# Two thirds of the modulation product moved from TensorE to GpSimd, and inputs laid out by the host

## What is computed

```python
def adaln_params(cond, w_mod, b_mod):
    m = jax.nn.silu(cond) @ w_mod + b_mod          # w_mod: 1024 x 6144
    return jnp.split(m, N_MOD, axis=-1)            # N_MOD = 6 parts of 1024
...
    sh1, sc1, g1, sh2, sc2, g2 = [m[:, None, :] for m in adaln_params(c, w_mod, b_mod)]
    csh1, csc1, cg1, csh2, csc2, cg2 = adaln_params(c_ctx, w_mod, b_mod)
    hc = rmsnorm(xc, n1) * (1 + csc1) + csh1
    ...
    h = rmsnorm(x, n1) * (1 + sc1) + sh1
    q, k, v, gb, gcv, u, ga, gv = split_proj(h @ w_in)
    ...
    x = x + g1 * merge_branches(y_attn, y_conv, ga, gv, w_mix_out)
    h2 = rmsnorm(x, n2) * (1 + sc2) + sh2
    x = x + g2 * peer(h2, pw_q, p_keys, p_u, p_v)
```

## Time and profile before

| | |
|---|---|
| runs | 1750.57, 1737.38, 1738.53 us; median 1738.53 |
| profiled execution | 1739.62 us, of which the span of instructions is 1737.8 us |
| busy | PE 1536.9 us, DVE 1044.2, ACT 774.4, POOL 276.6 |
| mean granted clock of PE | 0.953 of full speed |
| DMA | 431.63 MB, 248 GB/s over the span |

### The profile page before, as it was taken

One profiled execution on the slowest core, in us unless ns is written; L12 is line 12 of the kernel. 1 busy time (PEld: TensorE's weight loads), 2 busy tenths in 40 slices (PEclk: granted clock), 3 DMA queues, 4 the chain that ended last, 5 costly groups with the idle time before them and its releaser, 6 DMA issues.

```text
span 1737.8 us, 23096 instructions
## 1 busy us (share of the span) xinstructions
PE 1536.9 (88%) x8485; PEld 1124.3 (65%) x8485; DVE 1044.2 (60%) x2092; ACT 774.4 (45%) x1654; POOL 276.6 (16%) x260
## 2 busy tenths in 40 slices
PE   7899999969898898788877779888999988899997
PEld 4699559835444333222222249788999986899997
DVE  3445326466666666776665447535777766467774
ACT  2444333334444444444444353444555545455553
POOL 0000000035444443344444300000000000000000
PEclk9899999989999999999999989879999998899997
DMA  7345443399999999999999934303555531245551
GB/s 280 122 167 173 170 152 139 130 401 422 421 421 421 421 421 421 422 421 421 422 421 422 421 145 144 123 1 146 178 185 183 180 121 49 73 156 183 184 178 73
DMA packets 60724, 431.63 MB, mean 248 GB/s; under 512 B 6764, under 2 KB 7393, under 8 KB 8673
## 3 DMA queue, kind: packets, MB, share of 16 engines
q0 software_dynamic: 36864, 268.45, 37.2%
q1 hardware_dynamic: 22618, 159.51, 26.0%
q10 hardware_dynamic: 1159, 2.58, 0.5%
HBM read 429.47 MB, written 1.05 MB: 248 GB/s over the span
## 4 chain that ended last, share of the span: by engine, by line
PE 45%; DMA 20%; ACT 7%; DVE 5%; issue 2%; POOL 0%; ACTq 0%; POOLq 0%; DVEq 0%; SPq 0%
PE banks L595 18%; DMA arena<-in_peer_uv,experts 14%; PE banks L952 12%; PE banks L1058 7%; DMA tok_a<-in_peer_uv,experts 2%; DMA tok_b<-in_peer_uv,experts 2%; PE banks L834 2%; ACT diag L1330 2%; DVE wlow L1518 2%; PE banks L808 1%; PE banks L673 1%; PE banks L627 1%; ACT scores L1234 1%; ACT whigh L1099 1%; PE banks L792 1%
## 5 line engine op out<-in xcount | busy, mean ns | idle before, releaser
L952 PE MATMUL banks<-arena,diag 128*128 128x512 f32 x824 | 406.9, 631 | 99.1 <-ACT diag L1330 99.1
L952 PEld LDWEIGHTS banks<-arena,diag 128*128 128x128 f32 x824 | 150.9, 196 | 342.7 <-ACT diag L1330 207.9
L1871 DVE CUSTOM_DVE_ANT_0 arena<-arena,scores 128x1024 f32<-128x1024 f32 x206 | 252.6, 1226 | 191.7 <-DMA arena<-in_peer_uv,experts 190.9
L1518 DVE TENSOR_TENSOR wlow<-wring,whigh 128x1024 fp32r<-128x1024 f32 x234 | 275.4, 1219 | 128.9 <-ACT whigh L1099 128.9
L1472 POOL DMA_INDIRECT arena<-in_peer_uv,experts x206 | 221.9, 1077 | 648.3 <-DVE experts L1835 343.8
L1099 ACT ACTIVATE whigh<-wring 128x1024 fp32r<-128x1024 f32 x234 | 233.9, 1048 | 139.3 <-DMA wring<-in_w_qkv_a 33.6
L595 PE MATMUL banks<-f_high,whigh 128*128 128x256 f32 x720 | 206.0, 286 | 15.5 <-DVE f_low L1554 10.0
L595 PE MATMUL banks<-f_low,whigh 128*128 128x256 f32 x720 | 204.6, 284 | 0.0
L595 PE MATMUL banks<-f_high,wlow 128*128 128x256 f32 x720 | 204.5, 284 | 0.0
L1322 ACT ACTIVATE dots<-dots 128x1 f32<-128x1 f32 x256 | 51.4, 201 | 297.1 <-DVE dots L1871 296.6
L595 PE MATMUL banks<-a_high,whigh 128*128 128x256 f32 x552 | 165.8, 300 | 12.6 <-DVE a_low L1526 6.9
(11 more groups left out here) (251 smaller groups left out, 2525.6 us busy)
## 6 DMA issues: line engine op xcount, KB each, us to landing
wring<-in_w_up SPq DMA_DIRECT2D x44, 1024.0 KB, 4.8
wring<-in_w_mod SPq DMA_DIRECT2D x24, 1024.0 KB, 5.0
wring<-in_w_down SPq DMA_DIRECT2D x22, 1024.0 KB, 4.9
wring<-in_w_in SPq DMA_DIRECT2D x17, 1024.0 KB, 4.9
wring<-in_w_qkv_a SPq DMA_DIRECT2D x12, 1024.0 KB, 5.1
wring<-in_peer_w_q SPq DMA_DIRECT2D x8, 1024.0 KB, 4.9
wring<-in_w_mix_out SPq DMA_DIRECT2D x4, 1024.0 KB, 4.8
wring<-in_w_o_a SPq DMA_DIRECT2D x4, 1024.0 KB, 5.0
```

Source lines behind the costliest of these rows:

```text
L952: mm = nc.tensor.matmul(banks[:, 2 + 2 * b + half, :], diag[:, n % DIAGS, :], ring[n % RING][:, D + half * 512:D + (half + 1) * 512], star ...
L1518: V.tensor_tensor(low, w, high.bitcast(F32), ALU.subtract).then_inc(w_split, 1)
L1871: V.tensor_tensor_reduce(out=ring[n % RING][:, 0:D], in0=ring[n % RING][:, 0:D], in1=h2tok[:, b, :], scale=1.0, scalar=0.0, op0=ALU.mult, ...
```

## The change

Four things are done.

1. Modulation chunks 8 to 23 are computed by POOL for the one condition that is needed. POOL fetches each in two halves of 512 KB (`fetch`, two buffers at the end of `arena`), multiplies a half by `csil` broadcast along the columns (128 x 1024), and adds the four parts of a half and the two halves up: 7 operations a chunk, each waiting for the one before it (`link`). PE sums the result over the partitions with two matmuls of one column (`mod_columns`, line 686 of the change). POOL begins when PE has done chunk 6, and is at most two chunks ahead of PE (`mod_sum` has two buffers, `mod_made`).
2. PE takes the columns of chunks 8 to 13 behind projection steps 5, 7, 9, 11, 13 and 15, and those of chunks 14 to 23 in attention steps 0 to 9, where `mod_chunk` stood. `rows_out` is gone there; the expert stage has no modulation work and no w_mod load.
3. x and ctx come transposed from the host, straight into `xT` and `cT`; the vectors come as columns in three transfers; the keys come transposed straight into `cT` in one load of SP's list, between the loads of the projection chunks. PE's transposes and the copies behind them are gone. The sums of squares now stand behind chunk 2 and chunk 4, and DVE makes the rotary angles behind the first reciprocal.
4. SP's list begins with two w_mod chunks, then x, a third chunk, ctx.

```diff
+MOD_STEPS = [5, 7, 9, 11, 13, 15]
-MOD_ROWS = [88, 96, 104, 112]
+        mod_sum = sb("mod_sum", [P, 2, WIDE])
+        mod_half = arena[:, 56 * T:64 * T].rearrange("p (h n) -> p h n", h=2)
...
-        add_mods(MODS_1, MODS_2)
...
-        add_mods(MODS_2, MOD_TILES // 2)
...
+            while at < 2:
+                load(chunks[at]["slot"], chunks[at]["src"], chunks[at]["used"])
+                at += 1
+            sp.dma_start(xT[:, :, :].rearrange("p k t -> p (k t)"), a["x"]).then_inc(x_in, 16)
+            load(chunks[2]["slot"], chunks[2]["src"], chunks[2]["used"])
+            sp.dma_start(cT[:, :, :].rearrange("p k t -> p (k t)"), a["ctx"]).then_inc(ctx_in, 16)
...
+                    if c is in_chunks[5]:
+                        sp.wait_ge(h_ready, normed(1))
+                        sp.dma_start(cT[:, :, :].rearrange("p k t -> p (k t)"), a["peer_sub_keys"]).then_inc(keys_in, 16)
...
+            def mod_columns(i):
+                pe.wait_ge(mod_added, 7 * (i - MODS_1 + 1))
+                for j in range(2):
+                    t = 2 * i + j
+                    mm = nc.tensor.matmul(banks[:, 7, 2 * t:2 * t + 1], mod_sum[:, i % 2, j * P:(j + 1) * P], ones[:, 0:1],
+                                          start=True, stop=True)
+                mm.then_inc(mod_made, 1)
...
+                if i in MOD_STEPS:
+                    mod_columns(MODS_1 + MOD_STEPS.index(i))
...
-                    if which == 0:
-                        mod_chunk(MODS_1 + i)
+                    if which == 0 and MODS_1 + len(MOD_STEPS) + i < MODS_ALL:
+                        mod_columns(MODS_1 + len(MOD_STEPS) + i)
...
-                if n in MOD_ROWS:
-                    mod_chunk(MODS_2 + MOD_ROWS.index(n))
...
+            def fetch(half):
+                i, part = MODS_1 + half // 2, half % 2
+                pool.dma_start(mod_half[:, part, :], a["w_mod"][i * P:(i + 1) * P, part * CHUNK // 2:(part + 1) * CHUNK // 2]
+                               ).then_inc(mod_in[part], 16)
...
+            def link(ins):
+                nonlocal added
+                ins.then_inc(mod_added, 1)
+                added += 1
+                pool.wait_ge(mod_added, added)
+
+            pool.wait_ge(cond_ready, 1)
+            pool.wait_ge(mod_rows, MODS_1 - 1)
+            fetch(0)
+            fetch(1)
+            for half in range(2 * (MODS_ALL - MODS_1)):
+                i, part = MODS_1 + half // 2, half % 2
+                pool.wait_ge(mod_in[part], 16 * (half // 2 + 1))
+                if part == 0 and i >= MODS_1 + 2:
+                    pool.wait_ge(mod_made, i - 1)
+                total = mod_sum[:, i % 2, :]
+                w = mod_half[:, part, :].rearrange("p (k n) -> p k n", n=WIDE)
+                link(nc.gpsimd.tensor_tensor(w, w, csil[:, part * KT // 2:(part + 1) * KT // 2, 0:1].to_broadcast(
+                    [P, KT // 2, WIDE]), ALU.mult))
+                link(nc.gpsimd.tensor_tensor(w[:, 0:2, :], w[:, 0:2, :], w[:, 2:4, :], ALU.add))
+                if part == 0:
+                    link(nc.gpsimd.tensor_tensor(total, w[:, 0, :], w[:, 1, :], ALU.add))
+                else:
+                    link(nc.gpsimd.tensor_tensor(w[:, 0, :], w[:, 0, :], w[:, 1, :], ALU.add))
+                    link(nc.gpsimd.tensor_tensor(total, total, w[:, 0, :], ALU.add))
+                if half + 2 < 2 * (MODS_ALL - MODS_1):
+                    fetch(half + 2)
             for n in range(ROWS):
```

More of the change, by code:

```diff
@@ L698, in mod_chunk @@
                 c = mod_chunks[i]
-                started = i not in (0, MODS_1, MODS_2)
-                if started and mod_bank(i) == mod_bank(i - 1):
-                    mod_turn(i - 1)
                 pe.wait_ge(landed[c["slot"]], c["landed"])
@@ L880, in _ @@
                     g += 1
-            pe.wait_ge(keys_in, 16)
             pe.wait_ge(mod_ready, 2)
-            for n in range(4):
-                for j in range(4):
-                    mm = nc.tensor.transpose(banks[:, 4 + n, j * P:(j + 1) * P], keys[:, 4 * n + j, :], ident)
-                mm.then_inc(keys_turned, 1)
             for i, c in enumerate(mix_chunks):
@@ L1119, in _, with square @@
             norms = 0
-            def square(src, ready, count):
+            def square(src, ready, count, step=1):
                 nonlocal norms
@@ L1126, in square @@
                 for g in range(4):
-                    act.wait_ge(ready, count + g + 1)
+                    act.wait_ge(ready, count + (g + 1) * step)
                     nc.scalar.activation(hT[:, 2 * g:2 * g + 2, :], src[:, 2 * g:2 * g + 2, :],
@@ L1571, in _ @@
             dve.wait_ge(mod_made, MODS_1)
-            dve.wait_ge(vec_read, 1)
-            step.link(modulation(0, 2 * KT))
+            dve.wait_ge(vec_in, 16)
+            dve.wait_ge(x_in, 16)
+            dve.wait_ge(ctx_in, 16)
+            step.link(modulation(0, 2 * KT, 2))
             dve.sem_inc(mod_ready, 1)
@@ L1699, in _ @@
                 low_next()
-            dve.wait_ge(mod_made, MODS_2)
-            step.link(modulation(2 * KT, 5 * KT))
+            dve.wait_ge(mod_made, MODS_ALL)
+            step.link(modulation(2 * KT, 6 * KT, 1))
             dve.sem_inc(mod_ready, 1)
@@ L1909, in _ @@
                     if g * TOPK + s == TURN_ROW + 3:
-                        dve.wait_ge(mod_made, MOD_TILES // 2)
-                        step.link(modulation(5 * KT, MOD_TILES))
                         turned_in(0)
@@ L2090, with vectors @@
-NAMES = ["x", "c", "ctx", "c_ctx", "w_mod", "b_mod", "norm1_g", "norm2_g", "w_in", "attn_sink", "conv_w",
-         "w_attn_out", "w_conv_out", "w_mix_out", "peer_w_q", "peer_sub_keys", "final_g",
-         "positions_2", "attn_norm_2", "w_qkv_a_2", "w_o_a_2", "kv_norm_2", "w_kv_b_2", "w_q_b_2", "sinks_b_2",
-         "w_o_b_2", "ffn_norm_2", "w_up_2", "conv_w_2", "conv_b_2", "w_down_2", "final_norm_2"]
+def vectors(v):
+    order = [v["c"][0], v["c_ctx"], v["b_mod"][0], v["norm1_g"][0], v["norm2_g"][0], v["final_g"], v["conv_w"][0],
+             v["kv_norm_2"], v["final_norm_2"], None, v["attn_norm_2"], v["ffn_norm_2"], v["conv_b_2"], None,
+             v["conv_w_2"]]
+    rows, at = [], 0
+    for part, end in zip(order, [8, V_BMOD, V_N1, V_N2, V_FINAL1, V_CONV1, V_KVN, V_FINAL2, V_FINAL2 + KT, V_ATTN, V_FFN,
+                                 V_CONVB, V_CONVB + LAYERS * 2 * FF_TILES, V_CONVW, V_END]):
+        rows.append(np.zeros((end - at, P), np.float32) if part is None else part.reshape(end - at, P))
+        at = end
+    sinks = np.concatenate([v["attn_sink"][0], v["sinks_b_2"][0]])
+    return np.ascontiguousarray(np.concatenate([np.concatenate(rows).T, np.tile(sinks, (P, 1))], axis=1))
```

183 lines of the change are left out of this document (61 added, 122 removed).

## The result

The changed kernel takes 1770.7 us (median of 4 runs, 1767.99 to 1775.73), the kernel before 1737.95 us on the same chip. The ratio is 1.0153, with a 95% interval of 1.0109 to 1.0197: slower by 1.5%. The profiled execution is 1769.98 us, its span 1767.9, against 1737.8 before.

A forecast was written before the change was run, and what follows sets the result against it. POOL's nine attention chunks (113.4 us) were the new bound. Attention's start at 181.4 plus 113.4, 8 and 2 put the output product 43.8 us later; less 10 in the expert stage, 1739.6 became 1773 us, range 1733 to 1805.

The forecast's parts named there:

- the last rival: POOL's rate is three times DVE's per element: 4 us more a chunk, 1825 us; chance 0.20 together with shut-out engines.
- The start, -7: At the start, the last modulation turn ends at 47.8 instead of 54.9 us, 7 us earlier.
- A chunk on POOL, 12.6: One modulation chunk on POOL takes 12.6 us, at twice DVE's time per element, with links and two fetches.
- Two engines in the same memory, +6: POOL computing beside DVE in the scaling and at the convolution costs 6 us; bounds nothing to 18 and 12.
- The rival in which the engines shut each other out: DVE's two-input operations and POOL's wait for each other: up to 30 us, about 1800; chance 0.20 together with slower POOL.
- The rival's second part: Chunks in the projections take 2 us longer, so POOL comes 8 to 10 us late into attention.
- Ten waits of some 8 us: In attention, PE's column matmuls wait ten times for POOL, some 8 us each.
- The 31.5 us of PE's own work: In attention, PE's work without its twelve modulation chunks takes 31.5 us.
- the cheap rival: POOL at DVE's rate with nearly free fetches: 6.1 us a chunk, attention 55 us, time 1707 us; chance 0.10.
- Behind the last column, 8 and 2: From the last attention column to the output product: 8 us of remaining work, 2 us for PE's lower clock.
- Output product at 304.8: The output product behind the attention starts at 304.8 us instead of 261.0, 43.8 later.
- The expert stage, -10: In the expert stage, 4 MB of w_mod loads leave a full DMA, saving 10 us.

The follow-up runs named there:

- the kernel with operations of two columns: The changed kernel with POOL's seven operations per chunk cut to 2 of 256 columns, PE's columns taking the identity, modulation of chunks 8 to 23 left out: 1694.95 us.

## Why the prediction was right in its time, and where it was not

**1773 against 1770.7 us, inside the range, and "slower".** The bound is the one named: POOL's chain of nine chunks in the attention. But that it came within 3 us is luck, for errors of its terms cancel: the attention began 22.3 us later than forecast and was 15.9 shorter, and the expert stage was 9.7 shorter. (Two slips beside that: 1773.4 less the 1.1 us gives 1772.3, and the last rival adds up to 1829, not 1825. The forecast moves by less than 1 us for it.)

- *The start, -7*: -6.6. Right. The row that limits the first product is the load of the constants at 8.85 us and not chunk 0 near 6; chunk 2, with which the sum went on, was taken up at 17.9 (17.4 in the sum).
- *A chunk on POOL, 12.6*: 10.74, and that was the one rate that I chose. The additions over 512 and 256 elements (1.27 and 0.73) are 2.1 ns an element, as taken; the multiplication of 1024 with its broadcast operand is 1.91 us where 2.3 stood, the link 0.08 us and not 0.15, a fetch 0.89 and not 1.24. The estimate from the figure of the Trainium skill ("GPSIMD Engine Reference", section 3.1) was 12.0, too high as well. Nine chunks are 94.8 us (206.20 to 301.0) instead of 113.4.
- *Two engines in the same memory, +6*: **the term that failed.** It is 13.1 at the scaling (13.2 of it came back when POOL began later) and 15.4 at the convolution, 28.5 in all. Both lie inside the bounds written beside it (18 and 12) or just past them. The step that led to 6 was "DVE has slack in plain projection steps": DVE has none at the two places where PE waits for it. The rival in which the engines shut each other out had this mechanism right. The two scalings of the timeline above, 0.48 us each when alone, took 4.06 us together: a short operation pays for a whole long one. The rival's second part did not come: POOL was not late into the attention but waited 67.1 us for PE's columns in all. What stood against the rival, that DVE mostly reads PSUM in the attention, holds there (684 ns where 686 stood).
- *Ten waits of some 8 us*: ten waits, 3.5 on the mean and 6.1 at most. The time is POOL's either way, but PE's own work filled most of it, since the clock had fallen: weigh took 3.65 us where it took 2.00. The 31.5 us of PE's own work are 53.5 in the kernel with operations of two columns. That kernel also answers the cheap rival, which had 55 + 8 = 63 us from the start of the attention to the output product at 238: it takes 62.6 and gets there at 237.77, and POOL is not the bound in it. So that rival's stage could have come about; it failed on the price of a chunk, 10.74 us and not 6.1. Its 1707 lies 12 us above that kernel, and 9.6 of them are the expert stage.
- *Behind the last column, 8 and 2*: 10.1 (301.07 to 311.21). Right.
- *Output product at 304.8*: 311.21. Attention began 22.3 us later than forecast (203.7 against 181.4) and was 15.9 shorter.
- *The expert stage, -10*: -19.7. The four loads are 10.1 of it. The other 9.6 are a part of the change that the prediction did not look at for this stage: the inputs' layout from the host, 9.3 alone.

Beside -6.6, +28.5, and 1.4 for the columns and the takeover, the attention's +26.9 and the expert stage's -19.7 make 30.5, and the stages between and behind -0.4; the forecast had 33.8.

## What to carry to other kernels

An idle GpSimd is not free: before work is moved to it, look at what DVE does at the same time, and count each DVE operation with two operands in SBUF as the length of GpSimd's operation whenever something waits for DVE there. Give it such work where DVE reads PSUM or sleeps, or operations that only write. When work leaves TensorE and gaps come in its place, price the rest of its work at the lower clock too (0.68 and 0.65 in the two attentions with gaps, 1.00 before), and test the parts of a change apart: here the part that looked like housekeeping was worth some 16 us (6.5 and 9.3), and the main one cost 48 (1770.7 against 1722.48).

## What the runs showed of the hardware beyond that

- Reads on GpSimd against DVE: 0.48 us became 1.2 to 1.4, 0.69 up to 1.97, and 1.22 up to 2.0. An operation of two elements went from 0.16 to 0.75 on the mean. The operation with one tensor operand in SBUF suffered as well, 1.27 us on the mean for the four in the convolution (4.86 us together) where it takes 0.35 alone. Beside a memset there is one case, 0.54 us. The Trainium skill, "SBUF — State Buffer", section "Who interferes with whom", has VectorE contend with GpSimd in its two-port modes whatever GpSimd does; the one case agrees, if the operation ran in such a mode, which no run shows. In the other direction POOL's addition of 512 went from 1.27 up to 2.17 us and that of 256 from 0.73 up to 1.74, where the weights' split ran beside it (134 to 146 us).
- A plain fetch issued by POOL holds it for 0.59 us and 0.30 to the next; memsets on POOL took 0.96 us for 1024 elements, half of the multiplication.
- The rate of the gathers was 421 GB/s in every kernel with the old loads (four profiles) and 427 in all others (ten), whatever else was changed.
- PE's clock came back to 2.4 GHz within 5 us of PE's last wait in ten profiles. In four others (88, 88, 97 and 108 us) it stayed at 1.2 GHz through 23 to 25 us in which PE was busy without a gap, and the first takeover came 10 us later for it (91.67 against 81.37). What decides between the two stays open.
